# Banded attention in a fused encoder kernel: short end tiles packed, the group loop reordered, pooled products moved ahead

## The chip, the cores and the metric

The kernel runs on one core of one Trainium2 chip, as one launch. The metric is the device time of the launch in microseconds (us); the kernel before takes 2535.44 us (median of 3 runs, 2534.03 to 2535.8).

## The reference

A two-layer encoder trunk over 800 tokens in two sequences: 528 (16 meta tokens and 512) and 272 (16 and 256), model width 1024. Each layer is half a SwiGLU, a mixer, half a SwiGLU. The change is in the mixer of layer 0:

```python
z = h @ w_in                       # split into q | k | v | u (pooling input)
# banded attention: 8 heads of 64, 2 key/value heads, |t-s| <= 128
s = einsum(q, k) * 64**-0.5 - slope[head] * |t-s|        # outside the band: -1e30
m = max(max_s(s), sink[head])
p = exp(s - m);  denom = sum(p) + exp(sink[head] - m)
a = (p @ v) / denom
# pooling branch: 4 groups of 128 channels, windows 2, 4, 8, 16
pooled = centred_mean(u) - u
p = (pooled @ w_pool[group]) * pool_scale
h = h + concat([a, p]) @ w_out
```

## The kernel before, in words

All products of width 1024 run as three matmuls on fp32r operands (hi*hi, hi*lo, lo*hi), so every operand is split: ACT writes the hi part, DVE the lo part. PSUM is eight banks of 128 x 512 fp32. The order on each engine is written out by hand, in one block per engine (`block.sync`, `gpsimd`, `scalar`, `vector`, `tensor`), with semaphores between them; nothing is reordered by a planner.

Layer 0's mixer has three stages. First `w_in`: ten blocks of `square_block` (L1518), evacuated by DVE with the row norm. GpSimd (L555 to L583) computes the centred means of `u_pad` meanwhile. Then attention (PE L1655 to L1724, DVE L1355 to L1418, ACT L862 to L916), then the four pooled products (PE L1725, ACT L917, DVE L1419), then `w_out`: eight blocks of `square_block` on `mx_hi`, `mx_lo`, whose first four k-tiles are attention's output and whose last four are the pooled products.

Attention goes by query tiles of up to 128 tokens: 128, 128, 128, 128, 16 for the long sequence, 128, 128, 16 for the short one. Their keys number 256, 384, 384, 272, 144 and 256, 272, 144. A unit is one head of one tile: 64 units. Four units are a quad (`score_quad`, `norm_quad`, `exp_quad`), so a tile is two quads, and there are 16. A unit goes through

- PE `scores` (L1667): q times k into bank u % 4. Neighbouring units have their heads in different halves of the partitions;
- DVE L1369: adds the bias and takes the row maximum in one instruction; after four units `neg_max` (L1378) and `sink_d`;
- ACT `exp_quad` (L875): four exponentials with row sums, then `sink_e`;
- DVE `norm_quad` (L1392 to L1399): denominator, reciprocal, four multiplications;
- PE `transposes` (L1681): one 128 x 128 transpose per 128 keys, into bank 4 + u % 2;
- ACT `prob_copy` (L893, L896): from PSUM into `prob_t`;
- PE `times_v` (L1702), once for a tile, into bank 6 + i % 2; ACT `out_hi` (L903) and DVE `tile_lo` (L1406) split the result.

DVE's order is three maxima of quad q, `norm_quad(q-1)`, the fourth maximum, `neg_max`. ACT's order is four exponentials of quad q, four units of `prob_copy` of quad q-1. PE's order goes by pairs of units: two scores of pair u, two transposes of pair u - 8, and `times_v` of a tile behind the second pair of the tile after it. All of `scores(u)` to `scores(u+1)` wait until bank u % 4 has been read (`score_done`).

Of the kernel before, what the change touches and what calls it, by code (L numbers as in the profile page):

```python
# [8 lines left out]
P = 128  # L9
# [14 lines left out]
PAD = 8  # L24
# [7 lines left out]
HEAD_ORDER = (0, 4, 1, 5, 2, 6, 3, 7)  # L32
KEYS = 3 * P
# [185 lines left out]
def build(nc, x, gains, sinks, ident_in, alibi_in, edges_in, pool_w_in, tables, gate_up, down5, down6,  # L219
# [18 lines left out]
    def as32(ap):  # L238
# [42 lines left out]
    rest = 2 * XF - 2 * KD * T - projected - len(ATT_TILES) * P  # L281
    (_, xn_hi, xn_lo, q_sb, k_sb, v_sb, u_pad, v_tok, _, mx_hi, mx_lo) = scope([
# [3 lines left out]
        ("u_pad", [P, 4, POOL_W], f32), ("v_tok", [P, len(ATT_TILES), P], f32), ("fill_m", [P, rest], f32),  # L286
# [137 lines left out]
    def _(sp):  # L424
# [23 lines left out]
        for n, (what, cols) in enumerate(LOADS):  # L448
# [21 lines left out]
    v_tok_ps = sem("v_tok_ps")  # L470
    v_tok_done = sem("v_tok_done")
# [14 lines left out]
    pool_ps = sem("pool_ps")  # L486
    yx_zero = sem("yx_zero")
# [26 lines left out]

    UNITS = [(i, hd) for i in range(len(ATT_TILES)) for hd in HEAD_ORDER]

# [6 lines left out]
    def _(pool):  # L523
# [31 lines left out]
        pool.wait_ge(mix_in, 48)  # L555
# [71 lines left out]
    def _(act):  # L627
# [239 lines left out]
        def exp_quad(q):  # L867

            i = q // 2
            rows = ATT_TILES[i][3]  # L870
            k0, k1 = keys_of(i)
            act.wait_ge(neg_done, q + 1)
            for c in range(4):
# [5 lines left out]
            act.wait_ge(sinkd_done, q + 1)  # L879
            A.activation(sink_e[0:rows, q % 2, :], sink_d[0:rows, q % 2, :], ACT.Exp)\  # L880
                .then_inc(sink_e_done, 1)

        def prob_copy(u):
            i, hd = UNITS[u]
            side, c = divmod(hd, 4)
            rows = ATT_TILES[i][3]
            k0, k1 = keys_of(i)
            act.wait_ge(prob_t_ps, u + 1)
            if u % N_HEADS == 0 and i >= 2:
                act.wait_ge(tile_out, i - 1)  # L890
            full, kr = divmod(k1 - k0, P)
            if kr:
                A.activation(prob_t[0:kr, i % 2, side, full, c, 0:rows],  # L893
                             banks[0:kr, 4 + u % 2, full * P:full * P + rows], ACT.Copy)\
                    .then_inc(prob_t_done, 1)
            A.activation(prob_t[:, i % 2, side, 0:full, c, 0:rows],  # L896
                         banks[:, 4 + u % 2, 0:full * P].rearrange("p (j r) -> p j r", r=P)[:, :, 0:rows],
                         ACT.Copy).then_inc(prob_t_done, 1)

        def out_hi(i):  # L900
            s0, L, t, rows = ATT_TILES[i]
            act.wait_ge(tile_out, i + 1)
            A.activation(mx_hi[:, 0:4, s0 + t:s0 + t + rows],  # L903
                         banks[:, 6 + i % 2, :].rearrange("p (k r) -> p k r", k=4)[:, :, 0:rows],
                         ACT.Copy).then_inc(mix_hi_done, 1)

        NQ = len(ATT_TILES) * 2
        for q in range(NQ + 1):
            if q < NQ:
                exp_quad(q)  # L910
            if q >= 1:
                for c in range(4):
# [51 lines left out]
    def _(dve):  # L964
# [388 lines left out]
        dve.wait_ge(mix_in, 48)  # L1353

        def score_quad(q):  # L1355

            i = q // 2
            rows = ATT_TILES[i][3]
            k0, k1 = keys_of(i)
            off = k0 - (ATT_TILES[i][2] - P)  # L1360
            for c in range(4):
                u = 4 * q + c
                hd = UNITS[u][1]
                if c == 3 and q:
                    norm_quad(q - 1)
                dve.wait_ge(score_ps, u + 1)
                if u >= SCORES:
                    dve.wait_ge(prob_t_ps, u - SCORES + 1)
                V.tensor_tensor_reduce(out=score[0:rows, u % SCORES, 0:k1 - k0],  # L1369
                                       in0=banks[0:rows, u % 4, 0:k1 - k0],  # L1370
                                       in1=alibi[0:rows, hd, off:off + k1 - k0], scale=1.0,
                                       scalar=sink[0:rows, u % N_HEADS:u % N_HEADS + 1], op0=ALU.add, op1=ALU.max,
# [8 lines left out]
            hb = 4 * (q % 2)  # L1381
            V.tensor_tensor(sink_d[0:rows, q % 2, :], sink[0:rows, hb:hb + 4],
                            neg_max[0:rows, q % 2, :], ALU.add).then_inc(sinkd_done, 1)

        def norm_quad(q):

            i = q // 2
            rows = ATT_TILES[i][3]
            k0, k1 = keys_of(i)
# [12 lines left out]
        def tile_lo(i):  # L1402

            s0, L, t, rows = ATT_TILES[i]
            dve.wait_ge(mix_hi_done, i + 1)
            V.tensor_tensor(mx_lo[:, 0:4, s0 + t:s0 + t + rows],  # L1406
                            banks[:, 6 + i % 2, :].rearrange("p (k r) -> p k r", k=4)[:, :, 0:rows],
# [3 lines left out]
        NQ = len(ATT_TILES) * 2  # L1411
        for q in range(NQ):
            score_quad(q)
            if q >= 5 and q % 2 == 1:
# [534 lines left out]
```

## Time and profile before

| | |
|---|---|
| profiled execution, its own time | 2534.25 us |
| its span | 2532.2 us |
| TensorE (PE) busy | 2469.9 us (98%) |
| VectorE (DVE) busy | 1621.4 us (64%) |
| ScalarE (ACT) busy | 1001.3 us (40%) |
| GpSimd (POOL) busy | 80.7 us (3%) |
| mean granted TensorE clock | 0.984 |

The span is cut into 40 slices of 63.3 us; a digit is the busy share of a slice in tenths, and PEclk the granted TensorE clock in tenths of full speed (10 tenths stands as 9 too). Attention lies in slices 10 and 11 (counted from 0):

```profile
PE   9999999999789999999999999999999999999997
PEld 9999999999359999999999999999989899999996
PEclk9999999999889999999999999999999999999998
```

### The profile page before, as it was taken

The numbers are of one execution on the slowest core, as the hardware profiler recorded it, in microseconds if no ns is written. First come the engines' busy times: TensorE is split into PE (matmuls) and PEld (weight loads), VectorE is DVE, ScalarE is ACT, GpSimd is POOL, SyncE is SP. The second block draws the span as 40 slices with busy tenths as digits, with TensorE's granted clock in tenths as the row PEclk, the third lists the DMA queues.
The fourth block names the chain that finished last, engine by engine and source line by source line (L and its number), as shares of the span: only waits on it lengthen the run. The fifth ranks groups of instructions, "written<-read, shape, count | busy, mean of one in ns | idle before, by whom it ended". The sixth has DMA issues, their size and how long they took to land.

```text
span 2532.2 us, 35363 instructions
## 1 busy us (share of the span) xinstructions
PE 2469.9 (98%) x13780; PEld 2417.1 (95%) x13780; DVE 1621.4 (64%) x2858; ACT 1001.3 (40%) x1913; POOL 80.7 (3%) x85
## 2 busy tenths in 40 slices
PE   9999999999789999999999999999999999999997
PEld 9999999999359999999999999999989899999996
DVE  8675756753645857574767665765755876676574
ACT  6343433431644424252444333433443443343341
POOL 0000000024000000000000000000002100000000
PEclk9999999999889999999999999999999999999998
DMA  3212111121001121212121211121221211212121
GB/s 122 74 67 75 67 67 67 67 97 54 14 1 67 45 81 55 71 63 71 67 67 51 75 67 59 67 77 58 71 68 48 86 59 67 75 67 74 60 73 63
DMA packets 28533, 166.28 MB, mean 66 GB/s; under 512 B 3408, under 2 KB 3664, under 8 KB 16080
## 3 DMA queue, kind: packets, MB, share of 16 engines
q1 hardware_dynamic: 28368, 164.02, 18.7%
q8 instruction: 111, 1.82, 0.3%
q14 instruction: 54, 0.44, 0.1%
HBM read 160.73 MB, written 3.28 MB: 65 GB/s over the span
## 4 chain that ended last, share of the span: by engine, by line
PE 72%; issue 21%; DVE 4%; ACT 2%; DMA 0%; POOL 0%; POOLq 0%; SPq 0%; DVEq 0%; ACTq 0%
PE banks L1509 29%; PE banks L1588 12%; PE banks L1587 12%; PE banks L1586 12%; PE banks L1605 3%; PE banks L1502 2%; PE banks L1702 1%; ACT score L875 1%; DVE sum_sq_x L1023 1%; PE banks L1681 1%; ACT xf_hi L692 1%; PE banks L1667 0%; DVE xf_lo L1037 0%; DVE w_lo L991 0%; PE banks L1538 0%
## 5 line engine op out<-in xcount | busy, mean ns | idle before, releaser
L1587 PE MATMUL banks<-xf_lo,w_hi 128*128 128x400 f32 (+2 forms) x2240 | 766.9, 342 | 0.0
L1588 PE MATMUL banks<-xf_hi,w_lo 128*128 128x400 f32 (+2 forms) x2240 | 765.0, 342 | 0.0
L1586 PE MATMUL banks<-xf_hi,w_hi 128*128 128x400 f32 (+2 forms) x2240 | 764.2, 341 | 0.0
L648 ACT ACTIVATE w_hi<-raw 128x512 fp32r<-128x512 f32 (+3 forms) x572 | 314.8, 560 | 365.8 <-PE banks L1509 365.4
L1588 PEld LDWEIGHTS banks<-xf_hi,w_lo 128*128 128x128 f32 x2240 | 422.4, 189 | 0.0
L1587 PEld LDWEIGHTS banks<-xf_lo,w_hi 128*128 128x128 f32 x2240 | 420.4, 188 | 0.0
L1586 PEld LDWEIGHTS banks<-xf_hi,w_hi 128*128 128x128 f32 x2240 | 420.1, 188 | 0.0
L1509 PE MATMUL banks<-act_hi,w_lo 128*128 128x400 f32 (+2 forms) x1408 | 366.4, 341 | 0.0
L1509 PE MATMUL banks<-act_lo,w_hi 128*128 128x400 f32 (+2 forms) x1408 | 366.2, 341 | 0.0
L1509 PE MATMUL banks<-act_hi,w_hi 128*128 128x400 f32 (+2 forms) x1408 | 365.7, 341 | 0.0
L991 DVE TENSOR_TENSOR w_lo<-raw,w_hi 128x512 fp32r<-128x512 f32 (+3 forms) x572 | 344.3, 616 | 19.5 <-ACT w_hi L648 19.4
L648 ACT ACTIVATE w_hi<-w_sum 128x512 fp32r<-128x512 f32 x336 | 209.9, 629 | 300.0 <-DVE w_sum L983 117.7
L1509 PEld LDWEIGHTS banks<-act_hi,w_hi 128*128 128x128 f32 x1408 | 258.5, 188 | 0.0
L1509 PEld LDWEIGHTS banks<-act_hi,w_lo 128*128 128x128 f32 x1408 | 258.0, 188 | 0.0
L1509 PEld LDWEIGHTS banks<-act_lo,w_hi 128*128 128x128 f32 x1408 | 258.0, 188 | 0.0
L991 DVE TENSOR_TENSOR w_lo<-w_sum,w_hi 128x512 fp32r<-128x512 f32 x336 | 230.5, 689 | 0.6 <-ACT w_hi L648 0.6
L1178 DVE TENSOR_TENSOR act_lo<-act,act_hi 128x800 fp32r<-128x800 f32 (+2 forms) x88 | 86.2, 979 | 173.5 <-ACT act_hi L745 173.5
L1147 DVE SCALAR_TENSOR_TENSOR h<-banks,h 128x392 f32<-128x392 f32 (+3 forms) x224 | 72.6, 384 | 133.1 <-PE banks L1509 133.1
L1141 DVE SCALAR_TENSOR_TENSOR h<-banks,h 128x800 f32<-128x800 f32 x64 | 63.4, 990 | 134.4 <-PE banks L1509 134.4
L800 ACT ACTIVATE g<-banks 128x400 f32<-128x400 f32 (+2 forms) x80 | 40.1, 501 | 206.4 <-PE banks L1588 206.4
L975 DVE TENSOR_TENSOR w_sum<-raw 128x512 f32<-128x512 f32 x80 | 55.0, 688 | 81.3 <-PE banks L1509 50.5
L745 ACT ACTIVATE act_hi<-act 128x800 fp32r<-128x800 f32 (+2 forms) x88 | 75.3, 856 | 35.1 <-DVE act L1172 35.1
(181 smaller groups left out, 2660.1 us busy)
## 6 DMA issues: line engine op xcount, KB each, us to landing
raw<-gate_up_dram SPq DMA_DIRECT2D x86, 1024.0 KB, 4.8
raw<-down_dram SPq DMA_DIRECT2D x32, 768.0 KB, 4.3
raw<-down_dram SPq DMA_DIRECT2D x32, 640.0 KB, 3.8
raw<-w_in_dram SPq DMA_DIRECT2D x5, 1024.0 KB, 4.8
raw<-w_fourier_dram SPq DMA_DIRECT2D x8, 576.0 KB, 3.8
raw<-w_out_dram SPq DMA_DIRECT2D x4, 1024.0 KB, 4.8
h<-x_dram SPq DMA_DIRECT2D x8, 400.0 KB, 7.4
y_dram<-h SPq DMA_DIRECT2D x8, 400.0 KB, 2.5
```

What stands on the lines that cost most here:

```text
L648: A.activation(w_hi[:, n % NS, 0:u.cols], source, ACT.Copy).then_inc(w_hi_done, 1)
L745: A.activation(act_hi[:, t, 0:W], act32[:, t, 0:W], ACT.Copy).then_inc(act_hi_done, 1)
L975: ins = V.tensor_tensor(out, quarter(u, "A21"), quarter(u, "A22"), ALU.add)
L991: V.tensor_tensor(w_lo[:, n % NS, 0:u.cols], source, as32(w_hi[:, n % NS, 0:u.cols]), ALU.subtract).then_inc(w_ready, 1)
L1141: return V.scalar_tensor_tensor(two(h[:, m, :]), slot(2 + m % 2), 0.5, two(h[:, m, :]), ALU.mult, ALU.add)
L1147: last = V.scalar_tensor_tensor(h[:, m, t:t + n], banks[:, 4 + 2 * (m % 2) + half, c:c + n], 0.5, h[:, m, t:t + n], ALU.mult, ALU.add)
L1178: V.tensor_tensor(act_lo[:, t, 0:W], act32[:, t, 0:W], as32(act_hi[:, t, 0:W]), ALU.subtract).then_inc(act_ready, 1)
L1509: ins = M.matmul(banks[:, bank + half, 0:cols], a, b[:, half * cols:(half + 1) * cols], start=first and j == 0, stop=last and j == 2)
L1586: M.matmul(out, a_hi, b_hi, start=fresh and k == 0, stop=False, skip_group_check=True)
L1587: M.matmul(out, a_hi, b_lo, start=False, stop=False, skip_group_check=True)
L1588: ins = M.matmul(out, a_lo, b_hi, start=False, stop=k == KP - 1, skip_group_check=True)
L1605: ins = M.matmul(banks[:, bank + half, 0:C], a_lo if p == 2 else a_hi, b, start=kind[2] == "1" and k == 0 and p == 0, stop=kind[2] == "2" ...
```

## The change

- **Packing.** The two 16-token tiles go last. In each, the four heads of one side are stacked into 64 rows, so an end tile has two units instead of eight. Their queries are copied together by DVE into `q_end`; the bias and the sinks of stacked rows come as two more small inputs (`alibi_end`, `sink_end`). 52 units in 13 quads are left.
- **Loop order.** DVE takes all four maxima of quad q and `neg_max` before `norm_quad(q-1)`. ACT alternates: two exponentials of quad q, two copies of quad q-1, two exponentials, two copies.
- **Pooled products first.** PE issues scores 0 to 3 ahead of the transposes of v, then the four pooled products between scores 4 to 7. ACT (even groups) and DVE (odd groups) scale them from PSUM into `u_pad`; at the end ACT splits off `mx_hi` and DVE `mx_lo` from there. `w_out` waits for them only at its fifth k-tile.
- PE's loop starts with scores 8 and 9 and transposes 0 and 1; scores stay 8 units ahead.

```diff
+ATT_ORDER = [i for i, x in enumerate(ATT_TILES) if x[3] == P] + [i for i, x in enumerate(ATT_TILES) if x[3] < P]
+        for _side in range(2):
+            UNITS.append(AttUnit(_at, _i, _side, 0, 4 * END_ROWS, False))
...
 block.sync
-                for dst, src in ((alibi, alibi_in), (edges, edges_in), (pool_w, pool_w_in)):
+                sp.dma_start(sink_end[:, 0:4], sink_end_in[:, :]).then_inc(mix_in, 16)
+                for dst, src in ((alibi, alibi_in), (alibi_end, alibi_end_in), (edges, edges_in),
+                                 (pool_w, pool_w_in)):
...
 block.gpsimd
-        pool.wait_ge(mix_in, 48)
+        pool.wait_ge(mix_in, 80)
...
 block.scalar
+        def pooled_out(g):
+
+            act.wait_ge(pool_ps, g + 1)
+            sc = gain[:, len(NORMS) * KD + g:len(NORMS) * KD + g + 1]
+            A.activation(two(u_pad[:, g, 0:T]), slot(2 + g % 2), ACT.Copy, scale=sc).then_inc(pool_even, 1)
...
-        for q in range(NQ + 1):
-            if q < NQ:
-                exp_quad(q)
-            if q >= 1:
-                for c in range(4):
-                    prob_copy(4 * (q - 1) + c)
-                if q >= 4 and q % 2 == 0:
-                    out_hi((q - 4) // 2)
-        out_hi(len(ATT_TILES) - 1)
+        pooled_out(0)
+        for q in range(NQ + 1):
+            for first in (0, 2):
+                if q < NQ:
+                    exp_pair(q, first)
+                if q >= 1:
+                    prob_copy(4 * (q - 1) + first)
+                    prob_copy(4 * (q - 1) + first + 1)
+            if q == 0:
+                pooled_out(2)
+            if q >= 4 and q % 2 == 0:
+                out_hi((q - 4) // 2)
+        for at in range((NQ - 2) // 2, len(ATT_TILES)):
+            out_hi(at)
         for g in range(4):
-            act.wait_ge(pool_ps, g + 1)
-            sc = gain[:, len(NORMS) * KD + g:len(NORMS) * KD + g + 1]
-            A.activation(two(mx_hi[:, 4 + g, :]), slot(g % 2), ACT.Copy, scale=sc)\
-                .then_inc(mix_hi_done, 1)
+            if g == 1:
+                act.wait_ge(pool_odd, 2)
+            A.activation(mx_hi[:, 4 + g, :], u_pad[:, g, 0:T], ACT.Copy).then_inc(mix_hi_done, 1)
...
 block.vector
+        dve.wait_ge(in_evac, N_IN)
+        for n, i in enumerate(ATT_ORDER[-2:]):
+            s0, L, t, rows = ATT_TILES[i]
+            V.tensor_copy(q_end[:, n, :, :], q_sb[:, :, s0 + t:s0 + t + rows]).then_inc(q_end_done, 1)
...
-                if c == 3 and q:
-                    norm_quad(q - 1)
...
+        def pooled_out(g):
+
+            dve.wait_ge(pool_ps, g + 1)
+            sc = gain[:, len(NORMS) * KD + g:len(NORMS) * KD + g + 1]
+            V.tensor_scalar(two(u_pad[:, g, 0:T]), slot(2 + g % 2), sc, None, ALU.mult).then_inc(pool_odd, 1)
+
         for q in range(NQ):
             score_quad(q)
+            if q:
+                norm_quad(q - 1)
+            if q < 2:
+                pooled_out(2 * q + 1)
             if q >= 5 and q % 2 == 1:
                 tile_lo((q - 5) // 2)
         norm_quad(NQ - 1)
-        tile_lo(len(ATT_TILES) - 2)
-        tile_lo(len(ATT_TILES) - 1)
+        for at in range((NQ - 4) // 2, len(ATT_TILES)):
+            tile_lo(at)
         for g in range(4):
...
-            V.scalar_tensor_tensor(two(mx_lo[:, 4 + g, :]), slot(g % 2), sc,
-                                   two(as32(mx_hi[:, 4 + g, :])), ALU.mult, ALU.subtract)\
+            V.tensor_tensor(mx_lo[:, 4 + g, :], u_pad[:, g, 0:T], as32(mx_hi[:, 4 + g, :]), ALU.subtract)\
                 .then_inc(mix_ready, 1)
...
 block.tensor
+        for u in range(4):
+            scores(u)
+        for i, (s0, L, t, rows) in enumerate(ATT_TILES):
...
+        pe.wait_ge(pooled_done, 4)
+        pe.wait_ge(mix_in, 80)
+        pooled(0)
+        pe.wait_ge(score_done, 2)
+        scores(4)
+        scores(5)
+        pe.wait_ge(v_tok_done, len(ATT_TILES))
+        pooled(1)
+        pe.wait_ge(score_done, 4)
+        scores(6)
+        scores(7)
+        pooled(2)
+        pooled(3)
         AHEAD = 8
-        for u in range(0, NU + AHEAD, 2):
+        for u in range(AHEAD, NU + AHEAD, 2):
...
+            if v - 3 in LAST_OF:
+                times_v(LAST_OF.index(v - 3))
+        for at in range(len(ATT_TILES) - 2, len(ATT_TILES)):
+            times_v(at)
+        pe.wait_ge(prob_t_done, TCOUNT[-1])
+        pe.wait_ge(mix_ready, len(ATT_TILES))
         for m in range(KD):
             if m >= 2:
                 pe.wait_ge(out_added, m - 1)
-            square_block(WOUT[m], 4 + 2 * (m % 2), mx_hi, mx_lo)
+            square_block(WOUT[m], 4 + 2 * (m % 2), mx_hi, mx_lo,
+                         lambda kt: pe.wait_ge(mix_ready, len(ATT_TILES) + 4) if m == 0 and kt == 4 else None)
```

`pooled(g)` issues the same three matmuls as L1735 to L1739, into banks 4 and 5 (even g) or 6 and 7 (odd g); from g = 2 on it waits until the bank's group before has been scaled out. `LAST_OF[at]` is the last unit of a tile, so `times_v(at)` again follows the second pair of the next tile; that of the last full tile follows the last transposes.

## Rows read from the trace of the kernel before

**Rows 1.** The stretches by stage: w_in, attention, pooled products, w_out; busy time of each engine.

```profile
540.00:630.00 90.00, 89.32 (x498) 88.38 (x496) 31.54 (x47) 14.27 (x22) 40.76 (x35) 1.00 0.23 80
630.00:728.50 98.50, 74.40 (x376) 34.00 (x376) 60.95 (x266) 63.34 (x256) 0.00 (x0) 0.83 0.03 12
728.50:739.00 10.50, 7.92 (x28) 4.63 (x24) 4.98 (x6) 4.45 (x6) 0.00 (x0) 0.84 0.00 0
739.00:810.00 71.00, 70.99 (x383) 70.97 (x384) 29.11 (x41) 20.69 (x35) 0.00 (x0) 0.98 0.13 45
```

**Rows 2.** Waits by engine, 630 to 739 us: total, times, longest.

```profile
DVE score L1369 <- PE banks L1667: 24.0, 15, 4.0
PE banks L1681 <- ACT prob_t L896: 17.6, 10, 2.6
```

**Rows 3.** Chain of waits, 630 to 740 us: start, length, what.

```profile
635.16 0.40 DVE score L1369
635.80 2.07 ACT score L875 x8
643.93 1.58 PE banks L1667 x4
648.93 1.07 DVE score L1399 x3
650.01 0.53 DVE score L1369
650.78 2.50 ACT score L875 x8
658.18 0.85 PE banks L1667 x4
659.02 0.80 PE banks L1681 x6
668.10 4.11 PE banks L1702 x12
672.21 0.66 PE banks L1667 x4
714.28 1.87 PE banks L1702 x8
```

**Rows 4.** Timeline, attention: start, length, engine, instruction, idle before it.

```profile
630.40 0.20 PEld L1659 LDWEIGHTS banks<-ident,v_sb 128*128 128x128 f32 x2 [1.42 <-DVE q_sb L1349]
632.87 1.70 PE L1667 MATMUL banks<-k_sb,q_sb 64*128 64x256 f32 x8
633.26 1.28 ACT L875 ACT_TABLE_LOAD   x1
635.60 0.17 DVE L1378 TENSOR_SCALAR neg_max<-row_max 128x4 f32<-128x4 f32 x1
642.34 0.63 ACT L896 ACTIVATE prob_t<-banks 128x256 f32<-128x256 f32 x2
653.28 0.84 ACT L896 ACTIVATE prob_t<-banks 128x384 f32<-128x384 f32 x2
```

**Rows 5.** One-microsecond stretches: PE, PEld, DVE, ACT, POOL busy, clock, DMA.

```profile
704.00:705.00 1.00, 1.00 (x8) 0.71 (x8) 0.48 (x4) 0.61 (x3) 0.00 (x0) 0.50 0.00 0
714.00:715.00 1.00, 1.00 (x7) 0.34 (x6) 0.93 (x6) 0.89 (x5) 0.00 (x0) 1.00 0.00 0
```

**Rows 6.** Timeline, pooled products and the start of w_out.

```profile
733.35 0.94 PE L1735 MATMUL banks<-u_pad,pool_w 128*128 128x400 f32 x2 [0.17 <-DVE mx_lo L1422]
736.94 0.93 ACT L920 ACTIVATE mx_hi<-banks,gain 128x800 fp32r<-128x800 f32 x1 [1.01 <-PE banks L1739]
737.90 1.05 DVE L1422 SCALAR_TENSOR_TENSOR mx_lo<-banks,gain,mx_hi 128x800 fp32r<-128x800 f32 x1 [0.89 <-ACT mx_hi L920]
739.01 0.96 PE L1509 MATMUL banks<-mx_hi,w_hi 128*128 128x400 f32 x2 [2.10 <-DVE mx_lo L1422]
```

**Rows 7.** Timeline of GpSimd: its last pooling instruction.

```profile
596.09 2.50 POOL L581 TENSOR_TENSOR u_pad<-pool_a,u_pad 128x816 f32<-128x816 f32 x1
```

More of the change, by code:

```diff
@@ L32 @@
 HEAD_ORDER = (0, 4, 1, 5, 2, 6, 3, 7)
+ATT_ORDER = [i for i, x in enumerate(ATT_TILES) if x[3] == P] + [i for i, x in enumerate(ATT_TILES) if x[3] < P]
+END_ROWS = ATT_TILES[ATT_ORDER[-1]][3]
+END_KEYS = P + END_ROWS
+@dataclass
+class AttUnit:
+    at: int
+    tile: int
+    side: int
+    head: int
+    rows: int
+    full: bool
+UNITS = []
+LAST_OF = []
+for _at, _i in enumerate(ATT_ORDER):
+    if ATT_TILES[_i][3] == P:
+        for _hd in HEAD_ORDER:
+            UNITS.append(AttUnit(_at, _i, _hd // 4, _hd % 4, P, True))
+    else:
+        for _side in range(2):
+            UNITS.append(AttUnit(_at, _i, _side, 0, 4 * END_ROWS, False))
+    LAST_OF.append(len(UNITS) - 1)
+NU = len(UNITS)
+NQ = NU // 4
 KEYS = 3 * P
@@ L513, in cs_at, with prob_of @@
         return 10 * FOLD[0] + (2 * (tile - 5) + part) * FOLD[1]
-    UNITS = [(i, hd) for i in range(len(ATT_TILES)) for hd in HEAD_ORDER]
+    def prob_of(x, j):
+        part = prob_t[:, x.at % 2, x.side, j]
+        if x.full:
+            return part[..., x.head, :]
+        return part.rearrange("p j h r -> p j (h r)" if isinstance(j, slice) else "p h r -> p (h r)")[..., 0:x.rows]
     def keys_of(i):
@@ L865, in _, with exp_pair @@
                 .then_inc(v_tok_done, 1)
[L867 to L871, printed above, removed]
+        def exp_pair(q, first):
+            rows = UNITS[4 * q].rows
+            k0, k1 = keys_of(UNITS[4 * q].tile)
             act.wait_ge(neg_done, q + 1)
-            for c in range(4):
+            for c in (first, first + 1):
                 u = 4 * q + c
@@ L883, in prob_copy @@
         def prob_copy(u):
[L884 to L887, printed above, removed]
+            x = UNITS[u]
+            k0, k1 = keys_of(x.tile)
             act.wait_ge(prob_t_ps, u + 1)
-            if u % N_HEADS == 0 and i >= 2:
-                act.wait_ge(tile_out, i - 1)
+            if x.at >= 2 and UNITS[u - 1].at < x.at:
+                act.wait_ge(tile_out, x.at - 1)
             full, kr = divmod(k1 - k0, P)
@@ L892, in prob_copy @@
             if kr:
[L893 to L897, printed above, removed]
+                A.activation(prob_of(x, full)[0:kr], banks[0:kr, 4 + u % 2, full * P:full * P + x.rows],
+                             ACT.Copy).then_inc(prob_t_done, 1)
@@ L1699, in times_v @@
                 for side in range(2):
[L1700 to L1703 removed]
+                    part = slice(64 * side, 64 * side + 64)
+                    p = prob_t[0:kr, at % 2, side, j].rearrange("p h r -> p (h r)")
@@ L1704, in times_v, with pooled @@
+                    ins = M.matmul(banks[part, 6 + at % 2, 0:4 * rows], v_tok[0:kr, tile0 + j, part],
+                                   p[:, 0:4 * rows], start=j == 0, stop=j == n - 1)
             ins.then_inc(tile_out, 1)
         TCOUNT = [0]
-        for i, hd in UNITS:
-            k0, k1 = keys_of(i)
+        for x in UNITS:
+            k0, k1 = keys_of(x.tile)
             TCOUNT.append(TCOUNT[-1] + (2 if (k1 - k0) % P else 1))
-        NU = len(UNITS)
+        def pooled(g):
+            cut, b = L_PROMPT - TH, 4 + 2 * (g % 2)
+            if g >= 2:
+                pe.wait_ge(pool_odd if g % 2 else pool_even, 1)
+            M.matmul(banks[:, b, 0:TH], pool_w[:, g, :], u_pad[:, g, PAD:PAD + TH], start=True, stop=True)
+            M.matmul(banks[:, b + 1, 0:cut], pool_w[:, g, :], u_pad[:, g, PAD + TH:PAD + L_PROMPT],
+                     start=True, stop=True)
+            M.matmul(banks[:, b + 1, cut:TH], pool_w[:, g, :],
+                     u_pad[:, g, POOL_AT[1]:POOL_AT[1] + L_SAMPLE], start=True, stop=True).then_inc(pool_ps, 1)
```

175 lines of the change are left out of this document (87 added, 88 removed).

## The prediction

> **What bounds the kernel now.** I read the stretches by stage first. In w_in and w_out PE is busy without a gap (89.3 of 90.0 us, 71.0 of 71.0), so these and the SwiGLU stages can't answer to this change. From 630 to 739 us it is different: PE 76%, DVE 60%, ACT 62% over attention and pooled products together, and the granted clock is 0.83 [rows 1]. No engine is full there; what lasts is a ring of waits. The list of waits says which: DVE waited 24.0 us in 15 places for scores, and PE 17.6 us in ten places to start transposes (the list names the copies; what really came last was the norm before them) [rows 2]. The chain of waits shows one turn of the ring: multiplications of quad q-1, the fourth maximum, 2.50 us of exponentials of quad q, and again [rows 3]. Multiplications stand between the third and the fourth maximum, so the exponentials of q can't begin until those of q-1 have been finished, normalized and multiplied: one quad is in ACT and DVE at a time. Then `times_v` blocks PE for 4.11 us while the scores of the next maxima queue behind it. The clock adds to it: eight matmuls of `times_v` took 1.87 us at full clock (0.23 each), twelve took 4.11 (0.34 each) partly at half of it [rows 3, 5].
>
> **The path of the end.** PE is full from w_out on, so a microsecond by which w_out starts earlier than 739.01 [rows 6] is one off the kernel. I follow the new order from 630.40, the start of PE's first attention instruction [rows 4].
>
> **Front.** Scores 0 to 3: two pairs of at most 0.66 [rows 3], to 631.7. Transposes of v took 2.47 (630.40 to 632.87) [rows 4], to 634.2. A pooled group: from 733.35, where PE began the third, ACT took up the fourth at 736.94 [rows 6], 3.6 for two with a hand-over; I take 1.7 each. With scores 4 to 7 between, PE ends pooled(3) at 634.2 + 6.8 + 1.3 = 642.3. What it needs is there: GpSimd's last pooling instruction ended at 598.6 [rows 7]; two more small DMAs ahead of it in SP's queue and its own wait for all five have 35 us of cover. ACT scales group 0 first (0.93 [rows 6], to 636.8), loads its table (1.28 [rows 4], to 638.1), takes the exponentials of quad 0 (2.07 + 0.15, to 640.3). That is 2.3 us later than before: the first exponentials now queue behind a pooled product. DVE's two copies to `q_end` are new; between 0.17 (a 4-element instruction [rows 4]) and 0.53 (a maximum [rows 3]) each, at nothing, as ACT is not ready for quad 0 before 638.1. DVE: group 1 to 639.3 (0.93 to 1.05 for 800 elements, by the ACT and the DVE instruction of [rows 6]; I take 1.0), maxima of quad 1 to 640.9 (4 x 0.40 [rows 3]), `neg_max` 0.25, denominator and multiplications of quad 0 to 642.7 (0.4 + 3 x 0.36 and a start), group 3 to 643.7, maxima of quad 2 (4 x 0.53) and `neg_max` to 646.1.
>
> **Loop.** For a tile of 384 keys (two quads): PE 4 x (0.85 + 0.80) for pairs of scores and transposes plus 2.8 for `times_v` at full clock (12 x 0.234) = 9.4. ACT 2 x 2.50 + 4 x 0.84 for copies [rows 3, 4] + 0.6 for `out_hi` = 9.0. DVE 8 x 0.53 + 2 x 0.4 + 2 x 1.85 + 0.7 for `tile_lo` = 9.4. The exponentials of q now run beside the multiplications of q-1, and the maxima of q+1 need only scores. I followed one tile through the orders: maxima from 0, `neg_max` 2.4; norms of the quad before 3.3 to 4.35; its first copies 3.85, second exponential pair 4.75 to 5.95, `times_v` 5.85 to 8.65; the scores behind it come at 9.1 and 10.7 instead of 8.8, its transposes 9.4 to 10.2; ACT starts its next copies at 9.9 instead of 8.1. The next tile is then 10.2 behind this one: 1.09 times the largest engine sum. I use that factor for the others. From `neg_max` of quad 2 to that of 4: 9.9 (a `times_v` of eight matmuls); 4 to 6: 10.2; 6 to 8 (272 keys, scores 0.66): 4 x 1.46 + 2.8 = 8.6, so 9.4; 8 to 10 (256 keys, transposes two thirds as many): 7.6, so 8.2; 10 to 12 (272, ACT's 8.3 the largest): 9.0. Sum 46.7; `neg_max` of quad 12 at 692.8. Sixteen quads have become thirteen: the twelve units less are part of this.
>
> **Tail.** From there: two exponential pairs of stacked rows (64 x 144; between 0.17 and 0.63 an instruction, I take 0.40) between four copies and `out_hi`, 4.1 with a lag of 0.7; norm, transposes and copies of the last quad 4.0; `times_v` of the last full tile ends at 701.6; `out_hi`, `tile_lo` of it 1.35; then the last small tile may write its bank, 0.5, and its halves 0.5. w_out starts at 704.0. Its first four k-tiles are 24 matmuls of 0.185 (71.0 / 383 [rows 1]) = 4.4, to 708.4 at full clock. The four splits of pooled products lie beside them: ACT from 703.8, four of 0.93, DVE the last at 708.7 (1.0 more). A wait of 0.2; if the hi copies found no such cover, 4.7. The serial tail of pooled products, 10.5 us [rows 1], is gone, and its 6.8 us on PE stand in the front instead.
>
> **Clock.** The front is a mixture of short transposes and waits, as before. In the 98.5 us of attention the clock was 0.83 of full, so a third of it ran at 1.2 GHz, each time after PE had waited for norms. A denser loop has fewer of these waits. From both sides: none (0), or every `times_v` as slow as at 668.10 (5 x 1.3) and scores and transposes beside them. I take three of them and a slow front, 3 x 1.3 + 0.7 = 4.6.
>
> Sum: 739.0 - 704.0 - 0.2 - 4.6 = 30.2. The profiled execution took 2534.25, which gives 2504.0; the median is 1.2 above it: **2505.2**.
>
> **Rivals.**
> *Slow times_v (0.18).* The clock falls in each tile as now, and once for scores and transposes too: 6.5 + 6 in place of 4.6, 2513. For it: before, the clock fell with work on all sides as well. Against: the waits of 2 to 3 us ahead of transposes go.
> *The clock stays at half through the loop (0.08).* At 704 us PE was busy the whole microsecond with scores and transposes, at half clock; at 714 with `times_v`, at full [rows 5]. A pair of scores then costs 1.58 [rows 3], and if transposes double too, the tiles cost 16, 17, 16, 14 and 12 on PE: 75 in place of 46.7, with 2 in the front: 2505.2 - 4.6 + 30 = 2531. The Trainium skill (TensorE: Matmul & The Clock Gate, Part 4: PE-mode transpose) says that transposes don't count as PE-busy for the clock in the same way; the loop is over a third transposes. By that rule this case would be the likely one, at its 2531; the trace agrees only in part, since from 658 to 663 the same mixture took 0.85 and 0.80, full clock [rows 3].
> *The ring closes again (0.05), slower.* ACT alternates now, so its second exponentials queue behind copies, these behind transposes, these behind the norms that wait for exponentials. If a quad ran through all of it alone it would take 2.4 + 2.5 + 1.7 + 1.85 + 0.8 = 9.2 (384 keys), 8.1 (272) or 7.2 (256): 84 over ten quads, 37 more than 46.7: 2542. It decides against the change from 7.7 a quad on. Against it: the norm of q-1 needs only exponentials that ACT ended before the maxima of q.
> *The engines close up (0.11).* The loop at its largest engine sums (42.9) and no slow clock: 3.8 and 4.6 less, 2497.
>
> **How the numbers follow.** My own case has 0.58 and the range 2499 to 2511. The range for 8 in 10 takes in the closed-up engines and slow `times_v` and leaves out the others: 2496 to 2518. A change of 0.2% is 5.1 us, about what a measurement of this kernel tells from none. Half clock all through lies at its edge; I give it 0.05 to the same and 0.03 to faster. Faster 0.90, same 0.05, slower 0.05.
>
> **What would show it.** First exponentials near 638; `neg_max` some 5 us apart in the loop, ten for a tile of 384 keys; hardly any wait of PE for transposes above 1 us; clock above 0.9 in the stage; w_out starting 30 to 35 us earlier and no wait at its fifth k-tile above 1 us; every later stage as long as before. I am wrong if DVE still waits for scores more than 10 us in all, if the clock stays near 0.8 or below, or if w_out starts later than 720.

## The result, and the profile after

The changed kernel takes 2498.37 us (median of four executions, 2496.05 to 2501.64), the kernel before beside it 2535.62 (2534.03 to 2536.85): a ratio of 0.9854, 95% interval 0.9841 to 0.9866, 37.3 us faster. Forecast were 2505.2 and a gain of 30.2. The profiled execution is the fastest of the four, 2496.05 at a span of 2494.2, granted clock 0.992; before it was 2534.25 and 2532.2.

First the stretches of the changed kernel that answer to [rows 1]: w_in, attention with the pooled products in it, w_out; then two stretches of ten us out of the loop, and the end of attention (busy time of PE, PEld, DVE, ACT, POOL; granted clock; DMA).

```profile
540.00:630.00 90.00, 89.14 (x497) 88.19 (x495) 31.95 (x47) 14.28 (x22) 40.68 (x35) 1.00 0.23 82
630.00:702.90 72.90, 61.67 (x352) 30.50 (x352) 54.89 (x223) 55.88 (x209) 0.00 (x0) 0.99 0.05 15
702.90:774.00 71.10, 71.04 (x379) 71.02 (x380) 32.81 (x45) 23.93 (x40) 0.00 (x0) 0.96 0.13 45
...
640.00:650.00 10.00, 7.71 (x41) 3.58 (x39) 9.58 (x40) 8.25 (x30) 0.00 (x0) 1.00 0.00 0
660.00:670.00 10.00, 9.30 (x59) 4.85 (x59) 8.66 (x36) 8.48 (x30) 0.00 (x0) 1.00 0.00 1
...
701.00:704.00 3.00, 1.94 (x11) 1.69 (x12) 1.25 (x4) 1.63 (x3) 0.00 (x0) 0.53 0.00 0
704.00:708.00 4.00, 4.00 (x13) 3.95 (x13) 3.09 (x4) 2.15 (x4) 0.00 (x0) 0.50 0.00 0
```

The 109 us between w_in and w_out have become 73; w_out is about as long as it was. The busy time in them fell far less than that: ACT from 67.8 (the sum over the two stretches of [rows 1]) to 55.9, DVE from 65.9 to 54.9, PE from 82.3 to 61.7, a part of PE's by the clock, 0.83 before and 0.99 now. So 11 to 12 of the 36 us are work that is no longer done in this stretch on DVE and ACT, and the rest was their idle time. Not all of that work is gone: w_out's stretch has 32.8 us of DVE and 23.9 of ACT where it had 29.1 and 20.7, since the splits of the pooled products now lie beside it. In the loop, from 640 to 690 us, the three engines are busy for 7.7 to 9.6 of ten us, where [rows 1] has DVE and ACT under two thirds.

The list of waits from 630 to 703 us (total, times, longest) answers to [rows 2]:

```profile
PE banks L1740 <- DVE score L1454: 5.7, 6, 1.2
DVE mx_lo L1461 <- ACT mx_hi L949: 5.4, 2, 4.2
DVE score L1426 <- PE banks L1728: 4.6, 7, 1.1
DVE u_pad L1470 <- PE banks L1779: 3.9, 1, 3.9
ACT prob_t L940 <- PE banks L1762: 3.5, 1, 3.5
PE banks L1740 <- ACT prob_t L942: 2.0, 4, 1.1
```

DVE waits 4.6 us for scores where it waited 24.0, and PE ahead of the transposes 7.7 in ten places (5.7 for multiplications, 2.0 for copies), none above 1.2, where [rows 2] has 17.6 for copies alone, up to 2.6. What is left stands at the ends: 3.9 in the front, where DVE stands before a pooled product, 3.5 and 5.4 in the tail.

The timeline of the front and of two `neg_max` of the loop:

```profile
629.17 0.99 DVE L1398 SCALAR_TENSOR_TENSOR q_sb<-banks,rstd 128x800 f32<-128x800 f32 x1 [6.50 <-PE banks L1571]
635.27 0.93 ACT L930 ACTIVATE u_pad<-banks,gain 128x800 f32<-128x800 f32 x1 [1.15 <-PE banks L1779]
636.21 1.28 ACT L917 ACT_TABLE_LOAD   x1
637.51 0.51 ACT L917 ACTIVATE score<-score,neg_max 128x256 f32<-128x256 f32 x1
640.33 0.62 PE L1779 MATMUL banks<-u_pad,pool_w 128*128 128x272 f32 x2
...
658.44 0.17 DVE L1434 TENSOR_SCALAR neg_max<-row_max 128x4 f32<-128x4 f32 x1
662.86 0.17 DVE L1434 TENSOR_SCALAR neg_max<-row_max 128x4 f32<-128x4 f32 x1
```

The chain of waits through a tile of the loop and through the tail (start, length, what):

```profile
662.08 2.73 PE banks L1762 x12
664.81 0.66 PE banks L1728 x4
665.47 0.49 PE banks L1740 x3
665.98 0.87 ACT prob_t L942 x2
666.85 1.00 ACT score L917 x4
...
696.59 2.90 PE banks L1762 x12
700.60 0.83 DVE mx_lo L1461 x2
701.43 0.89 PE banks L1762 x8
```

In [rows 3] multiplications, the fourth maximum and all exponentials of one quad follow one another on the chain. Now the multiplications and maxima are off it in this tile: of the 9.6 us from 662.08 to the next `times_v` at 671.67 PE has 4.8, and ACT, with copies and exponentials in turn, nearly all of the rest. Twelve matmuls of `times_v` take 2.73, not 4.11.

### The profile page after: what moved, and what is told of

Same layout as the page of the kernel before. It is cut to its first block, busy times and chain, and to the rows that moved or that the text cites. A ratio compares the mean times of both kernels' runs of the same rounds, so it can differ in the third digit from the quotient of the medians.

```text
span 2494.2 us, 35149 instructions
## 1 busy us (share of the span) xinstructions
PE 2447.4 (98%) x13732; PEld 2406.7 (96%) x13732; DVE 1614.8 (65%) x2814; ACT 992.1 (40%) x1864; POOL 80.2 (3%) x85
## 4 chain that ended last, share of the span: by engine, by line
PE 73%; issue 21%; DVE 4%; ACT 1%; DMA 0%; POOL 0%; POOLq 0%; DVEq 0%; SPq 0%; ACTq 0%
PE banks L1571 29%; PE banks L1650 12%; PE banks L1649 12%; PE banks L1648 12%; PE banks L1667 3%; PE banks L1564 2%; PE banks L1762 1%; ACT xf_hi L735 1%; DVE sum_sq_x L1072 1%; DVE xf_lo L1086 0%; DVE w_lo L1040 0%; PE banks L1740 0%; PE banks L1600 0%; PE banks L1728 0%; PE banks L1610 0%
```

## The experiments

All are timed against the kernel before on the same chip; "slower" and "faster" below are differences of medians from the changed kernel's 2498.37, and differences of 2 to 3 us lie within the ranges. "w_out" is its start in the profiled execution, "quad 2" and "quad 12" are the starts of their `neg_max`.

| kernel | us, median (range) | ratio to before [95%] | quad 2 | quad 12 | w_out |
|---|---|---|---|---|---|
| changed | 2498.37 (2496.05–2501.64) | 0.9854 [0.9841, 0.9866] | 645.13 | 690.36 | 702.96 |
| undo_dve_order | 2513.77 (2512.03–2515.91) | 0.9913 [0.9899, 0.9928] | 646.91 | 704.83 | 717.6 |
| undo_act_order | 2501.1 (2500.72–2502.88) | 0.9865 [0.9848, 0.9881] | 645.02 | 693.46 | 707.5 |
| undo_both_orders | 2513.75 (2512.18–2517.62) | 0.9924 [0.9906, 0.9942] | 646.59 | 703.54 | 717.4 |
| undo_pooled_first | 2503.04 (2501.18–2505.2) | 0.9871 [0.9856, 0.9886] | 642.50 | 687.73 | 711.15 |
| undo_packing | 2503.98 (2501.56–2505.5) | 0.9873 [0.9859, 0.9888] | 645.45 | 690.68 | 710.7 |
| order_alone | 2511.09 (2510.21–2513.82) | 0.991 [0.9895, 0.9925] | 642.39 | | 716.6 |
| before_filled | 2536.6 (2529.67–2539.44) | 1.0002 [0.9991, 1.0013] | | | 743.3 |
| after_filled | 2499.45 (2499.09–2502.1) | 0.9859 [0.9846, 0.9873] | | 690.29 | 705.4 |
| better | 2498.72 (2493.8–2499.34) | 0.9855 [0.9839, 0.9872] | 645.66 | 690.91 | 703.94 |
| better_filled | 2496.91 (2495.51–2498.81) | 0.9849 [0.9836, 0.9863] | 645.66 | 690.79 | 703.49 |
| shifted | 2501.69 (2499.68–2503.32) | 0.9867 [0.985, 0.9883] | 647.78 | | 708.45 |
| better_aligned | 2490.5 (2488.53–2492.16) | 0.9825 [0.981, 0.984] | 644.55 | | 702.39 |

**The order on DVE** (the changed kernel with the norm between the third and the fourth maximum again).

```diff
             for c in range(4):
                 u = 4 * q + c
+                if c == 3 and q:
+                    norm_quad(q - 1)
                 dve.wait_ge(score_ps, u + 1)
@@
             score_quad(q)
-            if q:
-                norm_quad(q - 1)
```

> The changed kernel with DVE's old order alone: the normalization of quad q-1 between the third and the fourth maximum of quad q. Theory (an opened ring: the gain comes because the exponentials of q no longer wait for the multiplications of q-1): two quads of 384 keys go from 9 back to 11 to 13 us, the clock falls again inside the loop, 12 to 18 us slower than the changed kernel's 2498, so 2510 to 2516. Rival (less work: packing and the vanished tail made the gain, the orders are a detail): at most 4 us slower, 2502, clock full.

The first theory held. The edit gives back 15.4 us of the 37.3, the largest part of any single edit. Its chain of waits shows the ring of [rows 3] again, with the exponentials in two halves:

```profile
657.14 1.07 DVE score L1456 x3
658.21 0.53 DVE score L1428
658.78 0.18 DVE neg_max L1436
658.98 1.31 ACT score L917 x4
660.29 0.75 ACT prob_t L942 x2
661.04 1.19 ACT score L917 x4
...
663.18 1.07 DVE score L1456 x3
```

This turn is 6.04 us (657.14 to 663.18) for a quad, and PE is not in it. The ten quads from 2 to 12 take 57.9, in the changed kernel 45.2. The clock in that attention stage is 0.92, and `times_v` at 668.36 took 4.87 for twelve: with the ring the low clock is back in places.

**The order on ACT** (all four exponentials, then all four copies).

```diff
-            for first in (0, 2):
-                if q < NQ:
-                    exp_pair(q, first)
-                if q >= 1:
-                    prob_copy(4 * (q - 1) + first)
-                    prob_copy(4 * (q - 1) + first + 1)
+            if q < NQ:
+                exp_pair(q, 0)
+                exp_pair(q, 2)
+            if q >= 1:
+                for c in range(4):
+                    prob_copy(4 * (q - 1) + c)
```

> The changed kernel with ACT's old order alone: four exponentials of quad q, then four copies of quad q-1. Theory (opened ring): ACT's sum is the same and the normalization of q gets its exponentials earlier, so 0 to 3 us slower, 2498 to 2501. Rival (alternation is what keeps PE going, since the second pair of transposes needs the copies of the first): PE waits 1 to 2 us in each quad for copies, 8 to 12 us slower, 2506 to 2510.

2.7 us slower by the medians; the two intervals overlap, so the times alone don't settle it. The rival's 8 to 12 us are excluded. The marks of the profiled execution show a loss: quad 2 is as early as in the changed kernel, quad 12 is 3.1 later and w_out 4.5.

**Both orders undone** (the two diffs above together).

> The changed kernel with both old orders, DVE's and ACT's; packing and pooled products stay. Theory (DVE's order is the one that opens the ring, ACT's is a detail in either): as with DVE's old order alone, 2513.8, within 2 us. Rival (the two effects are separate and add up): 15.4 and 2.7 above the changed kernel, 2516.5. Rival (alternation only helps an open ring and harms a closed one): 3 to 6 us faster than DVE's order undone, 2508 to 2511.

2513.75, by the medians the same as with DVE's alone. The interval, 0.9906 to 0.9942, would allow the 2516.5 of the rival too; the marks are what speaks against it. With ACT's old order as well, the ten quads take 57.0 us, not 57.9, and w_out starts 0.2 earlier, where ACT's old order alone made it 4.5 later. So the order on ACT is worth something only once DVE's is there.

**The orders by themselves** (the kernel before, with the two new orders and nothing else; the diffs are the reverse of the two above).

> The kernel before with both new orders and nothing else of the change: 64 units, pooled products at the end. Theory (the orders carry half of the gain by themselves): 16 to 20 us faster than before, 2516 to 2520, with fewer stretches at half clock. Rival (the orders only pay once packing and pooled products are changed): at most 8 us faster, 2528.

2511.09, more than the 16 to 20 us that I expected: 24.5 us of the 37.3 come from moving these lines (23.9 against the kernel before as timed beside this run). The other 12.7 are the pooled products and the packing; undone one at a time below, these give back 4.7 and 5.6.

**Pooled products at the end** (the changed kernel with its packing and orders; the four pooled groups behind the last `times_v`, on banks 0 to 3, scaled where they are split, as before).

```diff
         for at in range(len(ATT_TILES) - 2, len(ATT_TILES)):
             times_v(at)
+        pe.wait_ge(pooled_done, 4)
+        pe.wait_ge(mix_in, 80)
+        pe.wait_ge(score_done, NU)
         pe.wait_ge(prob_t_done, TCOUNT[-1])
-        pe.wait_ge(mix_ready, len(ATT_TILES))
+        for g in range(4):
+            pooled(g)
+        pe.wait_ge(mix_ready, len(ATT_TILES) + 4)
...
```

> The changed kernel with the four pooled products back behind attention, as in the kernel before, and w_out waiting for all of them. Theory (the tail was a serial chain of PE, ACT and DVE, and its price in the front is about half of it): the tail of 10.5 us is back, the loop starts 4 us earlier, 6 to 7 us slower than 2498, so 2504 to 2505. Rival (PE's work was only moved): 2 us slower, 2500. Rival (all of the tail was gained): 10 us slower, 2508.

4.7 us slower, less than the 6 to 7 expected. Its chain of waits has the serial tail again:

```profile
694.06 4.29 PE banks L1760 x12
...
701.18 1.63 PE banks L1774 x2
...
709.08 0.94 ACT mx_hi L967
710.04 1.06 DVE mx_lo L1482
711.15 1.00 PE banks L1569 x4
```

10.0 us from 701.18 to 711.15. But quad 2 is 2.6 earlier than with the products in the front, and the 0.6 that PE waited for the last halves ahead of w_out lie within these 10.0 now. Against it, twelve matmuls of `times_v` took 4.29, partly at half clock, and not 2.90. That makes w_out 8.2 later. w_out itself, entered behind the pooled products, ran at full clock, while in the changed kernel its first 5 us were at half: to the next norm it takes 78.4 and not 80.7. So the profiled executions are 5.9 us apart at that norm; the 4.7 of the medians is less, by no more than the executions of one kernel differ.

**Packing** (the changed kernel with eight heads of 16 rows a short tile, sixteen quads).

```diff
-        for _side in range(2):
-            UNITS.append(AttUnit(_at, _i, _side, 0, 4 * END_ROWS, False))
+        for _hd in HEAD_ORDER:
+            UNITS.append(AttUnit(_at, _i, _hd // 4, _hd % 4, END_ROWS, True))
...
```

> The changed kernel with the two 16-token tiles as eight units each again, still at the end: 64 units in 16 quads. Theory (a quad costs its instructions, nearly whatever their size, 3.3 to 3.8 us for small ones): three quads more, 9 to 11 us slower, 2507 to 2509. Rival (small units hide beside times_v and the waits of the last full tile): 3 to 4 us slower, 2502.

5.6 us slower, between the 9 to 11 of the theory and the 3 to 4 of the rival: neither had the size right. It is the same to quad 12, then 20.0 to w_out and not 12.6: three quads more, whose short instructions wait for one another, and half clock from 697.9 to 701.2 (twelve matmuls of `times_v` took 4.57, not 2.90) and again from 704.6 into w_out.

**Is the clock cause or consequence?** The kernel before with two products of 128x384 that nobody reads, ahead of each quad's transposes, meant to give PE work while it waits for the norms.

```diff
+FILL = 2
@@
-            pe.wait_ge(norm_done, u + 1)
             if u >= 2:
                 pe.wait_ge(prob_t_done, TCOUNT[u - 1])
+            if u % 4 == 0 and u:
+                for _ in range(FILL):
+                    M.matmul(banks[:, 4 + u % 2, 0:KEYS], ident[:, :], alibi[:, 0, :], start=True, stop=True)
+            pe.wait_ge(norm_done, u + 1)
```

> The kernel before, with two products of 128 x 384 that nobody reads issued on PE ahead of its wait for the norms of each quad (1.3 us at full clock, 2.6 at half, into the bank that the transposes overwrite). They keep PE busy where it waited for norms. Theory (the low clock was a consequence of the closed ring): the clock stays higher, times_v is faster, but quads stay bound by ACT and DVE in turn: 2531 to 2537. Rival (the clock was itself the larger part of the loss): times_v at 2.8 and scores at 0.85 throughout, 10 to 15 us faster, 2521 to 2525.

The stretch from 630 us to w_out in that kernel (DVE waited 30.1 us in it for scores):

```profile
630.00:743.30 113.30, 94.74 (x460) 46.91 (x460) 66.12 (x271) 67.82 (x262) 0.00 (x0) 0.91 0.03 10
```

The clock rose from 0.83 to 0.91 and the kernel got no faster: the time is the one that the first theory expected. But the run doesn't decide the question. The fillers come where PE had little to wait for. Its long waits, at the third unit of a quad and for copies, are still there in good part (10.0 us in six places, where [rows 2] has 17.6 in ten), and the fillers lie on the chain themselves, eight pairs of 1.49 or 2.86 us, 14.7 in all, so what a higher clock gave may have been spent on them. One of the pairs:

```profile
659.77 1.49 PE banks L1681 x4
```

The trace of undo_dve_order says more. From 683 us to its quad 12 the clock is full, and the four quads from 8 to 12 take 20.9 us (683.91 to 704.83), in the changed kernel 18.3 (672.05 to 690.36):

```profile
683.00:704.83 21.83, 17.20 (x104) 7.93 (x100) 15.86 (x71) 15.49 (x62) 0.00 (x0) 1.00 0.00 1
```

So the ring costs time at full clock too. What the low clock added to it elsewhere, in the 7.8 us to quad 7 with its slow `times_v` for instance (5.1 in the changed kernel), isn't shown apart.

**Fillers in the tail** of the changed kernel (3 to 6 products of 128x128 at four places behind the last scores, read by nobody).

```diff
+FILLS = {46: 1, 48: 2, 50: 1, "end": 1}
...
+        def fill(n):
+            if n:
+                pe.wait_ge(score_done, NU)
+            for _ in range(3 * n):
+                M.matmul(banks[:, 2, 0:P], ident[:, :], ones[:, :], start=True, stop=True)
@@
+            fill(FILLS.get(u, 0))
             pe.wait_ge(norm_done, u + 1)
...
```

> The changed kernel with short products that nobody reads (three of 128 x 128 in fp32, some 0.65 us at full clock) on PE where it waits in the tail: one ahead of transposes 46 and 50, two ahead of 48, one ahead of w_out. In the changed kernel the clock fell at 701.3 and the first 6.7 us of w_out ran at half of it, which costs 3.3 us. Theory (the tail's idle PE costs clock where PE is alone on the path): the clock stays full into w_out, 2 to 3.5 us faster than 2498.4, 2495 to 2496. Rival (fillers only occupy PE, as in the kernel before, where they gained nothing): 0 to 2 us slower, 2499 to 2500.

No gain, as the rival had it: w_out started 2.4 later and the half clock came all the same, from 702.9 to 709.7.

**A shorter front and tail** (better): the transposes of v side by side in two banks with one wait for all, the table of the exponential loaded ahead of the v copies, and the packed tiles in one buffer with banks of their own, so that they need not wait for the last full tile. better_filled adds the fillers.

```diff
+    exp_first = sb("exp_first", [P, 4])
...
+        A.activation(exp_first[:, :], gain[:, 0:4], ACT.Exp)
...
-            if i >= 2:
-                pe.wait_ge(v_tok_done, i - 1)
-            M.transpose(banks[0:rows, 6 + i % 2, 0:P], v_sb[:, s0 + t:s0 + t + rows], ident[:, :])\
+            M.transpose(banks[0:rows, bank, col * P:(col + 1) * P], v_sb[:, s0 + t:s0 + t + rows], ident[:, :])\
...
-            if at >= 2:
+            if at >= N_FULL:
+                pe.wait_ge(score_done, NU)
+            elif at >= 2:
                 pe.wait_ge(mix_ready, at - 1)
...
```

> The changed kernel with a shorter front and tail. Front: the eight transposes of v go into two banks side by side and leave in four copies, without turns between PE and ACT, and a first exponential of four columns loads ACT's table while w_in runs. Tail: the two packed tiles share one buffer of prob_t and go to banks 0 and 1, so they wait neither for times_v nor for the split of the last full tile. If both chains set the time: neg_max of quad 2 some 1.5 to 2 us earlier than 645.1, w_out 1.5 us sooner behind the loop: 3 to 3.5 us faster, 2495. If the front is hidden behind ACT's later work: 1.5 us, 2497.

> The version with the shorter front and tail and the same fillers. In its profile the front was 1.5 us shorter, but the clock fell at 698, three microseconds earlier than in the changed kernel, so times_v of the last full tile and 5 us of w_out ran at half. Theory (front and tail are real gains that the clock took back): with fillers neg_max of quad 2 13.4 us behind the stage's first instruction, w_out 10.5 to 11.5 us behind neg_max of quad 12, w_out at full clock: 5 to 6 us faster than the changed kernel, 2492 to 2493. Rival (the fillers can't hold the clock in a tail of transposes): 2497 to 2499.

No faster than the changed kernel, where 3 us were expected of the first and 5 to 6 of the second, although the front is shorter: from the last evacuation of w_in to quad 2 it took 14.46 us, not 15.96. The tail is not: from quad 12 to w_out it took 13.03 us in better and 12.70 in better_filled, against 12.60. In better the clock fell at 698, and the last 28 matmuls of `times_v` took 6.23 us; in better_filled they took 3.92, but 4.3 us of its chain are fillers. So no run shows what the removed waits of the tail are worth alone. The two marks of better that were later, the last evacuation (631.20, not 629.17) and the stages behind w_out, lie where nothing of the edit runs. With fillers there is no half clock in the tail or in w_out:

```profile
690.79:703.49 12.70, 11.83 (x86) 6.99 (x82) 4.68 (x18) 7.51 (x37) 0.00 (x0) 1.00 0.00 1
```

The medians differ by 1.8 and the intervals overlap, so the times don't say whether the fillers pay. In the profiled executions the part that the edits touch did get shorter: from the last evacuation of w_in to the norm behind w_out the changed kernel takes 154.48 us, better 153.68 and better_filled 151.30 (the kernel before 189.61).

**The address of the operands.** What differed ahead of attention was one small tensor more, which moves the tensors allocated behind it by 32 bytes: `w_lo` from byte 75392 to 75424. Two kernels test it. shifted is the changed kernel with 32 unused bytes at that place; no instruction differs. better_aligned is better_filled with 64 bytes there (moved by 64 in all).

```diff
     var = sb("var", [P, KD])
+    pad_32 = sb("pad_32", [P, 8])
```

```diff
-    exp_first = sb("exp_first", [P, 4])
+    exp_first = sb("exp_first", [P, 16])
@@
-        A.activation(exp_first[:, :], gain[:, 0:4], ACT.Exp)
+        A.activation(exp_first[:, 0:4], gain[:, 0:4], ACT.Exp)
```

> The changed kernel with nothing but an unused tensor of 32 bytes a partition ahead of the large operands: w_lo stands at byte 75424 and not 75392, x_hi and x_lo as much later. No instruction differs. Theory (address): last evacuation of w_in at 631.2 in place of 629.2, the median matmul of w_in 345 and not 343 ns, and about 4 us more in all: 2502.4 (2501.5 to 2503.5). Rival (the address does nothing): 629.2 and 2498.4. Rival, half of it, if only w_in answers: 2500.4.

> As better_filled, except that the tensor of the early exponential takes 64 bytes a partition and not 16 (it was rounded to 32), so that the large operands behind it (w_lo, x_hi, x_lo) stand at byte addresses that are multiples of 64 again, as in the changed kernel (75456, and not 75424). Theory, the 32 bytes slowed every stage that reads these operands: better_filled ended its last evacuation of w_in at 631.2, 2.0 us later than the changed kernel's 629.2, and lost about 2 us more behind w_out, so this one ends it at 629.2, starts w_out near 701.5 and takes 4 us less: 2492.9 (2492 to 2494). Rival, the address does nothing, and the two us have another cause in the new front: last evacuation at 631.2 and 2496.9 again. Rival, only the part ahead of 630 answers to it: 2494.9.

Four marks of the timeline, the first matmuls of the norms and the last evacuation of w_in; the changed kernel:

```profile
29.71 1.57 PE L1600 MATMUL banks<-ones,sum_sq_x 128*100 128x1 f32 x16
...
783.65 1.49 PE L1600 MATMUL banks<-ones,sum_sq_x 128*100 128x1 f32 x16
1318.86 1.49 PE L1600 MATMUL banks<-ones,sum_sq_x 128*100 128x1 f32 x16
```

shifted:

```profile
30.41 1.57 PE L1601 MATMUL banks<-ones,sum_sq_x 128*100 128x1 f32 x16 [0.57 <-DVE sum_sq_x L1073]
631.82 0.99 DVE L1399 SCALAR_TENSOR_TENSOR q_sb<-banks,rstd 128x800 f32<-128x800 f32 x1 [6.58 <-PE banks L1572]
...
789.10 1.49 PE L1601 MATMUL banks<-ones,sum_sq_x 128*100 128x1 f32 x16
1325.92 1.49 PE L1601 MATMUL banks<-ones,sum_sq_x 128*100 128x1 f32 x16
```

better_aligned:

```profile
30.28 1.57 PE L1615 MATMUL banks<-ones,sum_sq_x 128*100 128x1 f32 x16 [0.57 <-DVE sum_sq_x L1087]
630.09 0.99 DVE L1413 SCALAR_TENSOR_TENSOR q_sb<-banks,rstd 128x800 f32<-128x800 f32 x1 [6.56 <-PE banks L1586]
780.61 1.49 PE L1615 MATMUL banks<-ones,sum_sq_x 128*100 128x1 f32 x16
1315.03 1.49 PE L1615 MATMUL banks<-ones,sum_sq_x 128*100 128x1 f32 x16
```

From the start of the first norm to that of the last evacuation the changed kernel takes 599.46 us, and so do the kernel before and eight variants without the added tensor, 599.45 to 599.49 in all ten. shifted takes 601.41, better and better_filled 601.42, better_aligned 599.81. The next full-speed stretch, from norm to norm, is 535.21 in the changed kernel and before, 536.82 in shifted, 534.42 in better_aligned. So the address does it: kernels with the same addresses agree within 0.04 us there, and these differences are more than eight times that.

Two things of the expectations failed. A multiple of 64 is not the rule: at `w_lo` = 75456 the first stretch is 0.35 longer than at 75392 and the second 0.79 shorter. And the loss isn't kept to the end: from the norm near 1850 us (in the changed kernel) to the end of the span shifted takes 643.3 us, the changed kernel 644.7 and the kernel before 647.3. The whole of shifted is 3.3 us slower by the medians, with overlapping intervals; of the 7.3 us between the two profiled executions another 2.8 lie in attention and w_out, where its tail fell to half clock already at 698. better_aligned is 7.9 us faster than the changed kernel by the medians, below the range that I expected, and its interval ends where the other's begins (0.984, 0.9841): it is the fastest version here. Of the 5.5 us between the spans of the two profiled executions 4.0 lie between the last evacuation and the norm behind w_out (150.52 and 154.48), where the front, the tail and the fillers are; the address is mixed into it, since w_out reads moved operands too.

## Why the prediction was right, and where its size was off

The measured 2498.4 lies inside the range for 8 in 10 and 0.6 below the range of my own case.

**What bounds the kernel: right.** The ring through the norm ahead of the fourth maximum was the limit. Undoing that one order brings it back (15.4 us), and the two new orders in the old kernel give two thirds of the gain. One reading under it was wrong. I took the norm for what PE's waits ahead of transposes really ended with; the list of waits, which names the copies, was right. This line is from the kernel before:

```profile
653.89 1.51 PE L1681 MATMUL banks<-ident,score 128*128 128x128 f32 x6 [2.38 <-ACT prob_t L896]
```

The multiplications of that quad had ended at about 650.0. The copies stood on ACT behind the four exponentials of the next quad, which ran from 650.78 to 653.28 [rows 3, 4]. The two new orders act on both: these exponentials start earlier, and the first two copies no longer wait for the last two of them.

**Front: right, somewhat long.** Forecast and measured: first exponential 638.1 and 637.51, PE ends the fourth pooled group 642.3 and 640.9, `neg_max` of quad 2 646.1 and 645.13. The first exponentials do queue behind a pooled product, 0.93, and the table load, 1.28. DVE's stand of 3.9 us ahead of pooled group 1 ended at 637.45, forecast 638.3.

**Loop: right.** Two-quad periods 9.9, 10.2, 9.4, 8.2, 9.0 were forecast, 46.7 in all; measured are 8.30, 9.43, 9.19, 9.53, 8.78, 45.2. Against the largest engine sums (42.9) that is a factor of 1.05, not 1.09. The sum is nearer than its terms: the first period was 1.6 shorter than forecast and the fourth 1.3 longer.

**Tail: short by 1.4.** 11.2 was forecast from `neg_max` of quad 12 to w_out, 12.6 measured. A wait that I had not seen is `ACT prob_t L940 <- PE banks L1762`, 3.5 us: the second packed tile shares its buffer with the last full tile, and its copies stand until `times_v` of that tile has ended. I let them be done by then; on the chain they are 0.6 us. The rest is the last full `times_v`, which ended 0.3 later than I had it behind quad 12, and the last small tile with its halves, 1.5 us at half clock where I had 1.0. That w_out started at 702.96, so near the 704.0 of the forecast, is in part luck: the front was 1.0 early, the loop 1.5, the tail 1.4 late.

**The wait at the fifth k-tile** (0.2): none. The first four k-tiles took 6.75 us and not 4.4, most of it at half clock, and the four hi copies (3.14 from 702.49) and the four subtractions (to 707.09) lay beside them.

**The clock: this is the term that was mis-sized.** I took 4.6 us for three slow `times_v` and a slow front. From 630 to 701 the clock never fell; every twelve matmuls of `times_v` took 2.73 to 2.90, within 0.1 of the 2.8 for full speed. It fell once, from 701.3 to 708, behind the idle time of the tail; w_out had 3.3 us at half clock near its start before (739.4 to 742.7) and has 5.1 now, and from its start to the next norm the kernel takes 80.69 where it took 79.96, so 0.7 us is what the clock costs more than before. The range for the clock had 0 at one end, and that end was the right one. I went by the rows of before, where PE was at half clock in the middle of work [rows 5]; such stretches followed on PE's waits (2.38 us before 653.89, then eight matmuls of `times_v` in 2.77), and the waits went.

The rival with the clock at half all through rested on the same mixture of scores and transposes, and the loop disproves it: 1.00 in each ten microseconds from 640 to 690, with six instructions of transposes for every four of scores in a tile of 384 keys. The row at 704 us [rows 5] was a weak witness for it: by the timeline PE did the `times_v` of the small tile there, and then scores, not transposes. The Trainium skill (TensorE: Matmul & The Clock Gate, Part 4: PE-mode transpose) says that a transpose doesn't count as PE-busy in the same way; that may hold for transposes by themselves, which no run here tried, but here the measurement decides: mixed with scores and `times_v` they did not bring the clock down.

**The remainder.** The profiled execution gained 38.2 us and I forecast 30.2. Of the 8.0: w_out 1.0 earlier (36 before its old start, just above the 30 to 35 that I gave as a sign), the wait at the k-tile 0.2, the clock 4.6 less 0.7, and 2.7 behind the norm near 1850 us, where the span's last part took 644.7 and not 647.3. Of these 1.3 are the last norm, whose sixteen short matmuls took 1.57 at full clock in this execution and 2.83 in that of before. The rest of the 2.7, 1.4 us, I can't place; it is within the range of executions. 0.2 is outside the span.

**The rivals.** Slow `times_v` and half clock: no. The ring closing again: no, DVE's wait for scores fell to 4.6. The engines closing up came nearest in time (2497); of its two halves the clock was right and the loop at its engine sums was not.

What I had not seen is that the changed order on ACT does nearly nothing by itself (2.7 us with DVE's, nothing without), and that the pooled products, whose serial tail was 10.5 us, return only 4.7: the front pays 2.6, and w_out, entered straight from the idle tail, begins at half clock. DVE's new order without ACT's in the kernel before was not run, so how the 24.5 us divide there is not shown.

## What to carry to other kernels

When a stage has no full engine, follow one item round the chain of waits: an instruction that finishes the last item, placed ahead of one that starts the next, makes the stage serial, and moving it can be worth more than all the work saved. If the clock is low behind such waits, price the new order from rows at full clock, and keep the low clock for the stretches that will still have waits, here the tail. And when an edit adds a tensor, compare a stage that it doesn't touch before judging it by the total.

## What the runs showed of the hardware

- Moving fp32r matmul operands by 32 bytes in their partitions, with the same instructions in the same order, lengthened 600 us of back-to-back matmuls by 1.95 us (0.33%) and the next 535 by 1.61; another 32 bytes made these 0.35 longer and 0.79 shorter than at first. Which operand's address matters, and by what rule, stays open; only tensors allocated behind the added one were moved, all together.
- Ten kernels with the same addresses repeated a 599 us stretch within 0.04 us, while whole executions of one kernel range over 2 to 10 us. A mark from a full-speed stretch shows what the total can't.
- Extra products raised the clock in the ring (0.83 to 0.91) and bought no time there, with 14.7 us of them on the chain; in the tail of after_filled (15.1 us from quad 12 to w_out) they did not hold it, and in the shorter one of better_filled (12.7) they did.
